# Seven block products in place of eight in the second projection of a two-block transformer kernel

## What is computed

```
xn = rms_norm(x3, norm_g_2)             # (2048, 1024)
u  = xn @ a_w_in_2                      # (1024, 2560): q 1024, k 256, v 256, z 1024
q, k, v, z = split(u)
out = windowed attention of q, k, v; result gated by silu(z); projected; added to x3; normed
```

## Time and profile before

| | us |
|---|---|
| median of 3 runs | 3098.73 (3097.25 to 3102.13) |
| the profiled execution, its own time | 3101.18 |
| its span in the profile | 3099.0 |
| TensorE busy | 2976.8 (96%) |
| VectorE busy | 1645.6 (53%) |
| ScalarE busy | 1199.0 (39%) |
| GpSimd busy | 723.8 (23%) |

### The profile page before, as it was taken

How to read it: one execution, slowest core, us unless ns; L and a number is a source line. 1 busy time by engine, 2 the same in 40 slices (tenths; PEclk the granted TensorE clock), 3 DMA queues, 4 the chain that set the end, 5 groups by cost and what they waited for, 6 DMA issues and landing times. The chain is left out here.

```text
span 3099.0 us, 47836 instructions
## 1 busy us (share of the span) xinstructions
PE 2976.8 (96%) x18522; PEld 2499.7 (81%) x18522; DVE 1645.6 (53%) x2633; ACT 1199.0 (39%) x2672; POOL 723.8 (23%) x584
## 2 busy tenths in 40 slices
PE   8999999999899999989999799899899999799998
PEld 7988889987687878879999678688788888677776
DVE  4466665000888888866666677433441100066665
ACT  3222221011776767765555322322221111255453
POOL 1243442110411010017542344300001101131111
PEclk9999999999899999999999899899999999899999
DMA  5212212223301010023332556332245542554342
GB/s 177 69 60 73 72 58 78 73 62 78 87 22 49 23 49 22 23 63 101 101 103 66 195 212 244 135 129 76 91 124 119 122 89 61 160 162 136 128 142 76
DMA packets 254331, 302.92 MB, mean 98 GB/s; under 512 B 19440, under 2 KB 201760, under 8 KB 250912
## 3 DMA queue, kind: packets, MB, share of 16 engines
q1 hardware_dynamic: 254112, 299.92, 32.1%
HBM read 190.38 MB, written 109.47 MB: 97 GB/s over the span
## 5 line engine op out<-in xcount | busy, mean ns | idle before, releaser
L981 DVE CUSTOM_DVE_ANT_0 d_e<-d_score,d_dist,d_slope 128x1024 f32<-128x1024 f32 x256 | 318.4, 1281 | 66.4 <-PE d_score L1043 66.1
L626 PE MATMUL p_acc<-p_h_hi,p_w_hi 128*128 128x512 f32 x768 | 299.6, 390 | 1.2 <-POOL p_w_lo L378 1.2
L626 PE MATMUL p_acc<-p_h_hi,p_w_lo 128*128 128x512 f32 x768 | 299.7, 390 | 0.0
L626 PE MATMUL p_acc<-p_h_lo,p_w_hi 128*128 128x512 f32 x768 | 298.8, 389 | 0.0
L908 ACT ACTIVATE d_e<-d_e,d_neg_top 128x2048 f32<-128x2048 f32 x128 | 257.1, 2008 | 80.4 <-DVE d_neg_top L990 80.0
L552 DVE RECIPROCAL p_root<-p_root 128x512 f32<-128x512 f32 x64 | 214.6, 3353 | 123.9 <-ACT p_root L443 123.9
L1066 PE MATMUL d_out<-d_v,d_w_t 128*128 128x128 f32 x2048 | 251.9, 277 | 0.0
L1066 PEld LDWEIGHTS d_out<-d_v,d_w_t 128*128 128x128 f32 x2048 | 241.3, 194 | 0.0
L626 PE MATMUL s_acc<-s_h_hi,s_w_hi 128*128 128x512 f32 x576 | 224.4, 390 | 0.0
L626 PE MATMUL s_acc<-s_h_lo,s_w_hi 128*128 128x512 f32 x576 | 224.1, 389 | 0.0
L626 PE MATMUL s_acc<-s_h_hi,s_w_lo 128*128 128x512 f32 x576 | 224.1, 389 | 0.0
(11 more groups left out here) (286 smaller groups left out, 6810.9 us busy)
## 6 DMA issues: line engine op xcount, KB each, us to landing
cols<-k_carry SPq DMA_DIRECT2D x64, 256.0 KB, 2.4
w_q<-q SPq DMA_DIRECT2D x15, 1024.0 KB, 7.7
k_carry<-in_w_in SPq DMA_DIRECT2D x14, 1024.0 KB, 6.1
k_carry<-x SPq DMA_DIRECT2D x27, 512.0 KB, 3.7
o_parts<-l_stage SPq DMA_DIRECT2D x192, 66.0 KB, 1.7
m_o<-o_parts SPq DMA_DIRECT2D x48, 264.0 KB, 5.8
k_carry<-cols SPq DMA_DIRECT2D x48, 256.0 KB, 4.7
rows<-k_carry SPq DMA_DIRECT2D x32, 256.0 KB, 2.2
```

What stands on the lines that cost most here:

```text
L626: mm = pe.matmul(acc[:, room], w_part[:, j, kt, ct * P:(ct + 1) * P], h_part[:, kt, tc * BANK:(tc + 1) * BANK], start=(kt == 0 and m == 0) ...
L981: dve.tensor_tensor_reduce(e[:, m % 3, s, half * HALF:(half + 1) * HALF], score[:, 2 * half:2 * half + 2].rearrange("p a b -> p (a b)"), d ...
```

## The change

The second projection is now `second_projection`, by the Strassen-Winograd scheme on blocks: the inner dimension is halved, the columns of a block (256) are halved, and the tokens of a group (1024) are halved; seven products of half blocks (`FORMS`) take the place of eight.

- Blocks go in pairs (`SWA_PAIRS`), two "sides" j; five pairs for the tokens 0 to 1023, then the same five for 1024 to 2047. So there are ten pairs and 70 products, numbered n = 7 g + form. A product is 12 matmuls of 512 tokens for each side, over an inner dimension of 512, in one PSUM bank of a side; banks alternate between two products.
- Token operands: seven forms of a group of 1024 tokens (`y_hi`, `y_lo`, 128x2048 each). Forms 0 and 1 are raw quarters; the others are sums and differences that VectorE makes (`sum_t1`, `sum_t2`). Tiles 0 to 7 are turned at the start, 8 to 15 inside the products 12 to 15. The second group's operands are written over the first's in the products 28 to 34.
- Weight operands: four quarters of 128x1024 for both sides (`place`), loaded per pair and group; VectorE makes four sums (`sum_s1` to `sum_s4`), ScalarE the high part (`make_x_hi`) and VectorE the low part (`make_x_lo`) of each form, three products ahead (`RING`), after product n - 3 has ended.
- Results: the first product is copied by ScalarE (`keep_p1`), the others are added on VectorE (`add_parts`, once a side, twice in form 4). Forms 1, 4, 5 and 6 end a result of 128x512, stored from one buffer a side (`out_hi`, `out_lo`): silu on ScalarE; or high part on ScalarE and low part on VectorE (`finish`); or, for "rows", turned by TensorE in the next product (`turn_rows`) and copied by VectorE (`keep_rows`). The next result of a side waits until the last is stored.
- The scale of tiles 7 to 15 is applied by ScalarE (`scale_rows`), their gain by VectorE on the turned tile (`keep_raw`). Tiles 0 to 6 are normed in the gate stage (`norm_next`), whose SP queue loads them.
- `next_loads` is issued after the store of product 67.

In the cut below the parts stand in this order: tables, SP's queue, ScalarE, VectorE's pieces and its whole order, TensorE, then the gate stage.

```diff
...
+SWA_PAIRS = [((6, "silu_cols"), (7, "silu_cols")), ((4, "split"), (0, "split_scaled")),
+             ((1, "split_scaled"), (2, "split_scaled")), ((3, "split_scaled"), (5, "rows")),
+             ((8, "silu_cols"), (9, "silu_cols"))]
+FORMS = 7
+QUAD_OUT = 4
...
+        k_half, c_half = slice(4 * (n % 2), 4 * (n % 2) + 4), slice((n // 2) * P, (n // 2 + 1) * P)
+        for j in range(2):
+            block = SWA_PAIRS[pair % len(SWA_PAIRS)][j][0]
+            sp.dma_start(self.w_raw[:, j, k_half, c_half], self.w_b[block][:, k_half, c_half]).then_inc(self.w_loaded[n], 16)
...
+    PLACE_OF_FORM = (0, 1, 0, 0, 2, 3, 1)
+    SUM_OF_FORM = {2: 2, 3: 4, 4: 1, 6: 3}
...
+    FINAL_OF_FORM = {1: 0, 4: 1, 5: 2, 6: 3}
...
+    y_need = ((4, 4, 8, 9, 10, 11, 12), (13, 14, 18, 19, 20, 21, 22))
+    turns_at = {12: (8, 9), 13: (10, 11), 14: (12, 13), 15: (14, 15)}
...
+            return acc[:, 2 * (n % 2) + j]
...
+            for n in range(PRODUCTS):
+                g, form = n // FORMS, n % FORMS
+                if form < 4 and g + 1 < PAIRS_IN_ALL:
+                    sp.wait_ge(x_lo_made, FORMS * g + form + 4)
+                    inputs.load_w(sp, g + 1, (0, 2, 3, 1)[form])
+                if n == FORMS:
+                    sp.wait_ge(y_lo_made, y_need[0][5])
+                    for t in range(8, 12):
+                        inputs.load_x(sp, t)
+                if n == FORMS + 2:
+                    sp.wait_ge(y_lo_made, y_need[0][6])
+                    for t in range(12, 16):
+                        inputs.load_x(sp, t)
+                if form in FINAL_OF_FORM:
+                    store(g, FINAL_OF_FORM[form])
+                if n == PRODUCTS - 3:
+                    sp.wait_ge(x_lo_made, PRODUCTS)
+                    sp.wait_ge(y_lo_made, y_need[1][6])
+                    next_loads(sp)
...
+                if m >= RING:
+                    act.wait_ge(acc_full, 2 * (m - RING) + 2)
+                act.activation(x_hi[:, m % RING], inputs.place(place), ACT.Copy).then_inc(x_hi_made, 1)
...
+                act.wait_ge(summed, sums(g, FORM_OF_FINAL[i], j))
+                if kind == "silu_cols":
+                    act.activation(out_hi[:, j], out_lo[:, j], ACT.Silu).then_inc(staged[j], 1)
+                else:
+                    act.activation(out_hi[:, j].bitcast(F32R), out_lo[:, j], ACT.Copy).then_inc(z_hi_made, 1)
...
+                dve.tensor_tensor(t2[:, t % 2], y_raw(3, t), y_raw(2, t), ALU.subtract).then_inc(t2_made, 1)
+                dve.wait_ge(t2_made, 4 * half + t + 1)
+                dve.tensor_tensor(y_raw(0, t), t2[:, t % 2], y_raw(0, t), ALU.subtract).then_inc(y_summed, 1)
+                dve.tensor_tensor(y_raw(1, t), y_raw(1, t), t2[:, t % 2], ALU.subtract).then_inc(y_summed, 1)
...
+                if form in FINAL_OF_FORM:
+                    dve.wait_ge(stored[j], emptied(g, FINAL_OF_FORM[form], j))
+                out, other = (None, (out_lo, u_a), (u_a, u_a), (u_b, u_a), (out_lo, u_b), (out_lo, u_b), (out_lo, u_a))[form]
+                dve.scalar_tensor_tensor(out=out[:, j], in0=bank_of(n, j), scalar=scale_of(g, j), in1=other[:, j],
+                                         op0=ALU.mult, op1=ALU.add).then_inc(summed, 1)
+                if form == 4:
+                    dve.scalar_tensor_tensor(out=u_a[:, j], in0=bank_of(n, j), scalar=scale_of(g, j), in1=u_a[:, j],
+                                             op0=ALU.mult, op1=ALU.add).then_inc(summed, 1)
+            def finish(g, i, j):
+                if kind_of(g, j) in SPLITS:
+                    dve.wait_ge(z_hi_made, hi_no[g, i, j])
+                    dve.tensor_tensor(out_lo[:, j].bitcast(F32R), out_lo[:, j], out_hi[:, j], ALU.subtract)\
+                       .then_inc(staged[j], 1)
+            def keep_rows(g, i, j):
+                r = row_no[g, i, j]
+                dve.wait_ge(row_turned, r + 1)
+                dve.tensor_copy(out_hi[:, j], aux[:, r % 2]).then_inc(staged[j], 1)
...
+            make_x_lo(0)
+            for t in range(4):
+                first_lo(t)
+            make_x_lo(1)
+            sum_s1(0)
+            sum_s2(0)
+            for t in range(4):
+                if t < 3:
+                    dve.wait_ge(raw_by_act, t + 5)
+                else:
+                    keep_raw(READY)
+                    dve.wait_ge(raw_by_dve, 1)
+                sum_t1(0, t)
+                sum_t2(0, t)
+                make_t2_lo(0, t)
+                if t >= 2:
+                    add_parts(1, t - 2)
+                if t == 1:
+                    make_x_lo(2)
+                    sum_s4(0)
+                    sum_s3(0)
+            make_x_lo(3)
+            make_y_lo(0, 3)
+            make_x_lo(4)
+            for n in range(2, PRODUCTS):
+                g, form = n // FORMS, n % FORMS
+                before = ((n - 1) // FORMS, FINAL_OF_FORM.get((n - 1) % FORMS))
+                for j in range(2):
+                    if before[1] is not None and kind_of(before[0], j) == "rows":
+                        keep_rows(before[0], before[1], j)
+                    if form >= 1:
+                        add_parts(n, j)
+                    if form in FINAL_OF_FORM:
+                        finish(g, FINAL_OF_FORM[form], j)
+                if 2 <= n <= 4:
+                    make_y_lo(0, n + 2)
+                m = n + RING
+                if m < PRODUCTS:
+                    make_x_lo(m)
+                    if m % FORMS == 1:
+                        sum_s1(m // FORMS)
+                        sum_s2(m // FORMS)
+                        sum_s4(m // FORMS)
+                    elif m % FORMS == 2:
+                        sum_s3(m // FORMS)
+                for t in turns_at.get(n, ()):
+                    keep_raw(t)
+                last = n - (SECOND - FORMS)
+                if n == 20:
+                    dve.wait_ge(raw_by_dve, NT - READY)
+                    sum_t1(1, ALL)
+                if last == 2:
+                    for t in range(4):
+                        sum_t2(1, t)
+                        make_t2_lo(1, t)
+                elif 0 <= last < FORMS:
+                    make_y_lo(1, last)
...
+                elif 6 <= t < 9:
+                    pe.wait_ge(raw_by_act, t - 1)
+                elif t >= 9:
+                    pe.wait_ge(raw_by_dve, t - 8)
...
+            def turn_rows(g, i, j):
+                r = row_no[g, i, j]
+                pe.wait_ge(summed, sums(g, FORM_OF_FINAL[i], j))
...
+                for j in range(2):
+                    if j == 0:
+                        pe.wait_ge(x_lo_made, n + 1)
+                        if g % len(SWA_PAIRS) == 0:
+                            pe.wait_ge(y_lo_made, y_need[half][form])
+                    if n == 1:
+                        pe.wait_ge(raw_by_act, 3)
+                    elif n >= 2 and form == 2:
+                        pe.wait_ge(p1_kept, 2 * g + j + 1)
+                    elif n >= 2:
+                        pe.wait_ge(summed, sums((n - 2) // FORMS, (n - 2) % FORMS, j) + ((n - 2) % FORMS == 4))
+                    for kt in range(4):
+                        for m, (x_part, y_part) in enumerate(((x_hi, y_hi), (x_hi, y_lo), (x_lo, y_hi))):
+                            mm = pe.matmul(bank_of(n, j), x_part[:, n % RING, j, kt], y_part[:, form, kt],
+                                           start=(kt == 0 and m == 0), stop=(kt == 3 and m == 2))
+                    mm.then_inc(acc_full, 1)
+                    if n == 0:
+                        for t in ((4, 5), (6,))[j]:
+                            transposes(t)
+                    if n == 1 and j == 0:
+                        transposes(7)
+                    if j == 0:
+                        for t in turns_at.get(n, ()):
+                            transposes(t)
+                        previous, of_form = (n - 1) // FORMS, (n - 1) % FORMS
+                        if n >= 1 and of_form in FINAL_OF_FORM:
+                            for side in range(2):
+                                if kind_of(previous, side) == "rows":
+                                    turn_rows(previous, FINAL_OF_FORM[of_form], side)
...
-                    swa_inputs.load_gain(sp)
-                    for n in range(2):
-                        sp.wait_ge(stored[n], 16)
+                    for n in (0, 1, 2, 3):
+                        swa_inputs.load_w(sp, 0, n)
+                    sp.dma_start(next_gain[:, :], row_on_all(swa_gain, P)).then_inc(next_gain_loaded, 16)
+                    swa_inputs.load_gain_t(sp, swa_gain)
+                    for n in range(4):
+                        sp.wait_ge(stored[n % 2], 16 * (n // 2 + 1))
                         swa_inputs.load_x(sp, n)
+                if t >= NT - 4:
+                    n = t - (NT - 8)
+                    sp.wait_ge(stored[n % 2], 16 * (n // 2 + 1))
+                    swa_inputs.load_x(sp, n)
...
+                if t >= NT - 4:
+                    n = t - (NT - 8)
```

(12 more changed lines are left out.)

## The result

| | before | after |
|---|---|---|
| median of the runs, us | 3097.99 (3092.4 to 3102.13, 4 runs) | 3129.23 (3127.9 to 3130.61, 4 runs) |
| span of the profiled execution | 3099.0 | 3126.1 |
| second projection, TensorE's first to last matmul | 465.07 | 480.34 |
| end of that stage to TensorE's next instruction | 8.03 | 16.13 |

The changed kernel is slower: ratio 1.0102, 95% interval 1.0085 to 1.0120. The forecast was 3104.6 with a range up to 3120: the time lies above it, and a loss of 0.2% was forecast where 1.0% came. That the sign of the likeliest case held says little, since the forecast stood at the edge between "within" and "slower".

The account below looks back on a forecast made before the run. TensorE, busy 96% of the span, was taken as the bound. Terms -66.6 + 20 + 13.5 + 18 + 14 + 7 = +5.9 us took the profiled 3101.2 to 3107.1, median 3104.6; range 3072 to 3120.

Parts of the forecast that it names:

- likeliest case: Whole kernel: the forecast itself, median 3104.6 us, own range 3093 to 3115, chance 0.42.
- "within" and "slower": Whole time against a 0.2% (6.2 us) threshold: no measurable change, chance 0.25; slower by more, chance 0.44.
- Gross gain: Second projection without waits: 70 products of 5.44 us plus turns, 398.5 us in place of 465.1, so -66.6.
- Start: Product 2 waits for VectorE's third token operand until 36 us; TensorE idles 12, then half clock; +20 us.
- Turns: Products 12 to 15: TensorE waits for VectorE to keep turned tiles 8 to 15; 5.9, 3.7, 1.7 us; +13.5 us.
- The clock's price: After each TensorE idle time over 3 us, half speed for 3.4 us was charged as 1.7 us lost.
- Rows: Pairs 3 and 8: with one output buffer a side, turned results wait for keeping and storing; +18 us.
- Token group: Second group's token sums and low parts on VectorE make products 33 and 36 wait 5.9 and 4.9 us; +14 us.
- Tail: Stage end: last results' stores land behind the next stage's tables; its first load comes about 9.5 us after TensorE; +7 us.
- At no cost: Extra gate-stage norms, weights read twice, SP's weight loads waiting for low parts, and POOL's lost splits were claimed to cost nothing.
- VectorE keeps up: Faster rival: the three middle places' 45.5 us of waits halve (3082 us) or all go (3059); chance 0.33.
- Stores set the pace: Slower rival: slow store landings stop TensorE in every split pair, 4.3 us in some four pairs, 3122 us; chance 0.23.

Follow-up runs that it names:

- early loads: Against the changed kernel, only the loads of tiles 8 to 15 moved, from products 7 and 9 to 5 and 6 in SP's queue; 3120.66 us, ratio 1.0062.
- turns spread: Changed kernel with tile loads 8 to 15 moved earlier and those tiles turned in products 9, 10, 14 and 16; 3103.34 us, ratio 1.0007.
- token group spread: Changed kernel with second group's tile sums behind products 30 to 33, one each, and low parts of forms 3 to 6 behind 34 to 37; 3116.81 us, ratio 1.0053.
- eight variants: The eight follow-up kernels, all starting from the changed one, seven with parts of the queue order edited and one with all edits; medians 3069.47 to 3129.29 us.
- rows later: Changed kernel with "rows" additions waiting only for the previous turn, and results turned, copied and stored later; 3103.98 us, ratio 1.0010.

## Why the prediction was wrong

The terms of its sum, in its own order:

- **Gross gain, −66.6: right.** 5.44 us a product stood in every pair without a wait, 0.227 us from matmul to matmul. The 215.7 ns from start to start (the Trainium skill, "TensorE: Matmul & The Clock Gate", section "Wait — 56ns, not 53.3ns?") is not what this kernel's matmuls do in either trace.
- **Start, +20: 1.5 more.** Product 2 began 37.6 us after TensorE's first instruction, 36 was predicted; product 3 at 44.6 against 43.1.
- **Turns, +13.5: the step that failed.** It counted from the end of product 11 and gave VectorE's queue as addition, copy, low part, with no wait for a store. That product 11's own store would land unhindered was taken from the earlier trace rows, although the part on the tail, a few lines on, works out from the earlier trace rows what loads issued just ahead of a store do to it. The loads stand in the diff, behind product 9. Measured: 6.5 us more in that wait, and with the clock a term of 21.3. The experiment with early loads brought the wait back to 6.0. Apart from that the term was too small by its own rule: its parts add up to 13.3, and the wait of 3.7 at product 14, over 3 us, was charged no clock; it cost 1.8.
- **The clock's price: mis-sized.** 1.7 us per wait was read from one place (the row gives 3.1 to 3.2 us at half clock, so 1.6) and charged only where a wait was over 3 us. In this trace the matmuls after waits of 2.3 and 2.5 us (at 2408.38 and 2230.21) also ran at half clock, and lost 1.6 and 1.9; after the one of 3.8 at product 36 they lost 3.1. Over the stage 17.1 in place of 10.2. That, not the waits, is most of the miss in the next term.
- **Rows, +18: 25.7.** Five of the six waits were within 0.6 us of the prediction. The first of pair 8 was 2.8 where I had 1.3, since I let it have less to catch up than in pair 3.
- **Token group, +14: 12.8.** The two waits were shorter by 1.6 and 0.9, the clock cost more: the near hit is two errors that cancel.
- **Tail, +7: 8.1.** The mechanism, the queue and the last addition's wait for the stores behind the tables are all in the trace.
- **At no cost: held in time, but one reason is wrong.** "Those low parts are made before the results are" doesn't hold for form 1. VectorE's queue has the result of product 8 first and the low part of product 11's operand behind it, and SP's queue has the weight load that waits for this low part ahead of the store:

```profile
2300.21 0.69 DVE L1023 TENSOR_TENSOR s_out_lo<-s_out_lo,s_out_hi 128x512 fp32r<-128x512 f32 x1 [0.70 <-ACT s_out_hi L890]
2303.16 1.22 DVE L941 TENSOR_TENSOR s_x_lo<-k_carry,s_x_hi 128x1024 fp32r<-128x1024 f32 x1 [0.26 <-ACT s_x_hi L842]
2304.41 0.93 SPq L677 DMA_DIRECT2D k_carry<-in_a_w_in  x2
2305.39 1.51 SPq L181 DMA_DIRECT2D k<-s_out_hi  x2
```

The result's first side was complete at 2300.90 and its store went out 4.5 us later. Product 11's addition waited 0.9 us for it, and SP reached the loads behind product 9 only at 2312.01, just ahead of product 11's result. With the early loads the store of product 8 was as late (complete at 2286.70, issued at 2291.17) and no addition waited for it: alone the delay costs nothing. What share it has in the wait of 8.2 us, no run separates.

The stage came out 480.3 where 464.0 was predicted, 16.3 over: turns 7.8, rows 7.7, start 1.5, the token group −1.2, and 0.5 of small things. With 1.1 of the tail, 2.2 ahead of the stage and 1.5 after it, the span was 21.1 us over, and the profiled execution's own time 20.8 (3127.9 against 3107.1). The other 3.8 of the 24.6 lie between that execution and the median, which stood 2.5 below it before and stands 1.3 above it after.

Of the rivals, "VectorE keeps up" fell: all the waits that were forecast came. "Stores set the pace" fell as worked out (forms 4, 5 and 6 of the undisturbed pairs hold 5.44 us), but its time, 3122, came nearer, and its mechanism, a landing slowed by loads ahead of it in the queue, is the very one that decided in product 11. It was priced as a steady pace and acted once. The range was too narrow by the same step: its upper end took the bounds of each wait but not that of two queues meeting, and put no spread on a clock's price read in one place.

## What to carry to other kernels

Count for each wait not only the queue of the engine that is late, but the DMA queue that releases it: write down what is issued in the 5 us ahead of every store on whose landing something waits, and put large loads elsewhere. Reckon behind each pause of TensorE, of 2.3 us and more here, with a price in clock, and give it a spread: in these traces it lay between nothing and 3 us. An operation-saving scheme with enough throughput on every engine can lose all its gain to the order of the work; here the same arithmetic in another order went from 1.0% slower to 1.1% faster.

## What was unexpected of the hardware

- A pause of 2.3 us could put the matmuls behind it at half clock: the granted clock was 1.00 in the stretch before it and 0.53 in the one behind it (2405 to 2408.3 and 2408.4 to 2412, above). After pauses of 1.3 and 1.4 us (turns at 2434.21 and 2360.33) it stayed at 1.00. The row below is the first of these, a stretch that begins with the pause's end.

```profile
2434.20:2437.80 3.60, 3.59 (x18) 3.03 (x19) 3.53 (x4) 0.00 (x0) 0.00 (x0) 1.00 0.34 63
```

- A pause of that length did not always do so. With the turns spread, the one at product 23 was 3.1 us long, and the clock stayed at 1.00 in it and behind it (rows below). With the token group spread, it stayed at 1.00 after the pause of 2.3 us at product 58; and after the first product's pause of 2.46 us, the same in the changed kernel and all eight variants, it fell in six of these nine traces and stayed in three. What decides is not shown.

```profile
2386.92 0.66 PE L1117 MATMUL s_aux<-k_ident,s_out_lo 128*128 128x128 f32 x4 [3.10 <-DVE s_out_lo L1014]
...
2386.90:2390.00 3.10, 3.08 (x16) 2.64 (x17) 2.29 (x3) 0.00 (x0) 0.00 (x0) 1.00 0.38 106
```

- Two stores of 128 KB took 3.72 us of the queue behind 3 MB of loads, 1.25 behind the 1 MB of weights alone, and the median from issue to landing was 5.6 us in place of 3.3. The rows are of the view of DMA issues, around the stores of product 11, in the changed kernel and in the one with the early loads (times, KB each, median us to landing):

```profile
k<-s_out_hi SPq DMA_DIRECT2D x2, 128.0 KB, 5.6
```

```profile
k<-s_out_hi SPq DMA_DIRECT2D x2, 128.0 KB, 3.3
```

- Identical code far ahead of the change took some 14 us less in some executions. In the first block's attention the granted clock was then 0.99 in place of 0.97; here is the same window of the changed kernel and of the one with the rows later. What sets it is open; no run was made for it.

```profile
740.00:1240.00 500.00, 475.03 (x3663) 398.74 (x3661) 404.49 (x669) 342.98 (x547) 92.03 (x65) 0.97 0.16 43
```

```profile
740.00:1240.00 500.00, 483.17 (x3783) 405.08 (x3782) 409.01 (x689) 353.43 (x567) 92.09 (x65) 0.99 0.17 44
```
